# A layer's expert weights on one core: moved side work, and doubles that change places at every second step

## The reference, cut to what matters

```python
def _moe(h, w_router, b_router, w_gate, w_up, w_down):
    logits = (h @ w_router).astype(jnp.float32) + b_router.astype(jnp.float32)
    top_vals, top_idx = lax.top_k(logits, TOP_K)
    wts = jax.nn.softmax(top_vals, axis=-1)
    combine = jnp.sum(jax.nn.one_hot(top_idx, N_EXPERTS, dtype=jnp.float32) * wts[..., None], axis=-2)
    combine = combine.astype(h.dtype)
    out = jnp.zeros_like(h)
    for e in range(N_EXPERTS):
        out = out + combine[..., e:e + 1] * _swiglu(h, w_gate[e], w_up[e], w_down[e])
    return out
```

## Time and profile before

| what | value |
|---|---|
| median of 3 runs | 1944.58 us (1942.08 to 1948.06) |
| the profiled execution's own time | 1946.7 us |
| its span in the profile | 1944.6 us |
| TensorE busy | 1879.9 us, 97% |
| VectorE, ScalarE busy | 955.1 us, 743.2 us |
| moved by DMA | 488.11 MB, mean 251 GB/s |

### The profile page before, as it was taken

One profiled execution on the slowest core, in us unless ns is written; L12 is line 12 of the kernel. 1 busy time (PEld: TensorE's weight loads), 2 busy tenths in 40 slices (PEclk: granted clock), 3 DMA queues, 4 the chain that ended last, 5 costly groups with the idle time before them and its releaser, 6 DMA issues.

```text
span 1944.6 us, 30547 instructions
## 1 busy us (share of the span) xinstructions
PE 1879.9 (97%) x12510; PEld 1455.2 (75%) x12510; DVE 955.1 (49%) x1313; ACT 743.2 (38%) x931; POOL 127.6 (7%) x171
## 2 busy tenths in 40 slices
PE   7999999998999999999999998999999999999997
PEld 5999999997999988999999974356556655455444
DVE  4467554555444445575545642255455544333333
ACT  4434333445434334343334441244444443333222
POOL 2200001400000003000014010000000000000000
PEclk9999999999999999999999999999999999999999
DMA  9635356673666645533566739999999999899986
GB/s 359 212 122 162 112 171 178 201 271 88 192 211 184 231 125 166 160 109 103 163 195 206 238 142 365 384 387 380 402 395 387 381 409 373 306 324 353 349 311 232
DMA packets 275921, 488.11 MB, mean 251 GB/s; under 512 B 16951, under 2 KB 169657, under 8 KB 275778
## 3 DMA queue, kind: packets, MB, share of 16 engines
q1 hardware_dynamic: 266368, 458.02, 67.7%
q0 software_dynamic: 9392, 28.05, 4.7%
q10 hardware_dynamic: 18, 0.04, 0.0%
HBM read 473.45 MB, written 12.59 MB: 250 GB/s over the span
## 4 chain that ended last, share of the span: by engine, by line
PE 80%; DMA 8%; DVE 5%; SPq 2%; ACT 2%; issue 2%; POOL 1%; DVEq 0%; ACTq 0%; POOLq 0%
PE ps L2571 12%; PE ps L2572 11%; PE ps L2617 10%; PE ps L3291 6%; PE ps L3300 3%; DMA mraw<-in_w_exp_up 3%; PE ps L2641 3%; PE ps L3220 2%; PE ps L3443 2%; PE ps L2650 2%; PE ps L2538 2%; DMA mraw<-in_w_exp_down 2%; PE ps L3336 2%; PE ps L3250 2%; PE ps L3337 2%
## 5 line engine op out<-in xcount | busy, mean ns | idle before, releaser
L820 DVE TENSOR_TENSOR wlo<-raw,whi 128x1024 fp32r<-128x1024 f32 x244 | 288.9, 1211 | 310.7 <-ACT whi L1853 309.8
L2571 PE MATMUL ps<-h1h,whi 128*128 128x320 f32 x1248 | 384.8, 321 | 7.5 <-DVE h1l L927 3.9
L2572 PE MATMUL ps<-h1l,whi 128*128 128x320 f32 x1248 | 370.0, 309 | 0.0
L1853 ACT ACTIVATE whi<-raw 128x1024 fp32r<-128x1024 f32 x244 | 248.0, 1046 | 118.7 <-PE ps L2961 44.9
L2571 PEld LDWEIGHTS ps<-h1h,whi 128*128 128x128 f32 x1248 | 234.7, 188 | 23.6 <-issue 17.6
L1427 DVE TENSOR_TENSOR mhi<-mraw,mhi 128x2048 fp32r<-128x2048 f32 (+1 forms) x70 | 151.9, 2170 | 171.0 <-ACT mhi L2151 167.9
L2572 PEld LDWEIGHTS ps<-h1l,whi 128*128 128x128 f32 x1248 | 234.9, 188 | 0.2 <-issue 0.2
L2617 PE MATMUL ps<-h1h,wlo 128*128 128x320 f32 x1248 | 209.4, 310 | 0.0
L2151 ACT ACTIVATE mhi<-mraw 128x2048 fp32r<-128x2048 f32 (+1 forms) x70 | 127.0, 1814 | 205.0 <-DMA mraw<-in_w_exp_up 138.3
L2617 PEld LDWEIGHTS ps<-h1h,wlo 128*128 128x128 f32 x1248 | 189.0, 188 | 0.8 <-issue 0.8
L1658 DVE TENSOR_TENSOR mhi<-mraw,mhi 128x2048 fp32r<-128x2048 f32 (+1 forms) x35 | 75.9, 2168 | 120.6 <-PE ps L3342 115.4
(11 more groups left out here) (522 smaller groups left out, 3020.6 us busy)
## 6 DMA issues: line engine op xcount, KB each, us to landing
mraw<-in_w_exp_down SPq DMA_DIRECT2D x176, 512.0 KB, 10.2
raw<-in_w_in SPq DMA_DIRECT2D x128, 512.0 KB, 3.9
mraw<-in_w_exp_gate SPq DMA_DIRECT2D x123, 512.0 KB, 9.8
mraw<-in_w_exp_up SPq DMA_DIRECT2D x123, 512.0 KB, 11.3
raw<-in_w_ada SPq DMA_DIRECT2D x64, 512.0 KB, 3.9
mraw<-in_w_exp_gate SPq DMA_DIRECT2D x59, 384.0 KB, 7.3
mraw<-in_w_exp_up SPq DMA_DIRECT2D x59, 384.0 KB, 9.6
pause<-in_w_ada SPq DMA_DIRECT2D x32, 512.0 KB, 6.9
```

The source lines that it names most:

```text
L820: V.tensor_tensor(WLO[:, u % RAW_UNITS, 0:w], RAW[:, u % RAW_UNITS, 0:w], WHI[:, h % HI_UNITS, 0:w].bitcast(F32), ALU.subtract).then_inc(l ...
L1853: A.activation(WHI[:, h % HI_UNITS, 0:w], RAW[:, u % RAW_UNITS, 0:w], ACT.Copy).then_inc(hi_made, 1)
L2571: M.matmul(out_, w, v[0], start=start, stop=False, skip_group_check=True)
L2572: M.matmul(out_, w, v[1], start=False, stop=False, skip_group_check=True)
```

## The change

1. `triple_order`: `ahead` is 61 in place of 60. From pair 10 of the wide expert on, some narrow pairs stand one place earlier, and narrow pair 58 comes before wide pair 34. Behind wide pair 34 then stand the narrow pairs 59 to 69, where before it was 58 to 69.
2. `triple_units`: the combine units 5, 6 and 7, until now behind places 8, 9 and 10 of `ORDER`, stand behind places 10, 11 and 12.
3. ScalarE: the four GT copies are in a function that is called at pair 12 of job 0.
4. The doubles: at odd steps the wide pair comes first and the narrow one second, on TensorE and in the loads (narrow, wide, wide, narrow, and so on). The numbers that tell slots and counts follow.

```diff
-def triple_order(ahead=60):
+def triple_order(ahead=61):
...
-        units[3 + d].append(("combine", d))
+        units[3 + d if d < 5 else 5 + d].append(("combine", d))
...
-        return self.job * PAIRS - len(ASIDE) + self.stride * (p + 1) - 1
+        return self.job * PAIRS - len(ASIDE) + self.stride * (p + 1) - 1 - p % 2
...
-        return self.job * PAIRS - len(ASIDE) + self.stride * p
+        return self.job * PAIRS - len(ASIDE) + self.stride * p + p % 2
...
+            def wide_place(q):
+
+                return (q + q // 2) % 2
+
             def slot_free(both, q):
 
-                if q % 2:
+                if wide_place(q):
                     sp.wait_ge(m_lo, both.order * PAIRS + (q // 2 + 1))
                 else:
                     sp.wait_ge(m_used, both.job * PAIRS + (q + 1))
...
-                    load_pair((both.job * PAIRS - len(ASIDE) + q) % RAW_RING, experts[q % 2], q // 2)
+                    load_pair((both.job * PAIRS - len(ASIDE) + q) % RAW_RING, experts[wide_place(q)], q // 2)
...
-            act.wait_ge(hd_stored, 16 * TT)
-            act.wait_ge(sem("gt_in"), 1)
...
+            def gate_rows_out():
+
+                act.wait_ge(hd_stored, 16 * TT)
+                act.wait_ge(sem("gt_in"), 1)
...
+                    if side is SIDE_FIRST and p == 12:
+                        gate_rows_out()
...
+                    for part in (wide_, narrow) if p % 2 else (narrow, wide_):
+                        part()
```

More of the change, by code:

```diff
@@ L2185, in _ @@
             A.activation(*first_fill(0), ACT.Copy).then_inc(xe_out, 1)
-            act.wait_ge(hd_stored, 16 * TT)
-            act.wait_ge(sem("gt_in"), 1)
[L2188 to L2192, removed]
+            def gate_rows_out():
+                act.wait_ge(hd_stored, 16 * TT)
+                act.wait_ge(sem("gt_in"), 1)
+                for h in range(2):
+                    A.activation(GT[:, 0, 512 * h:512 * h + 512], PS[:, GT_BANKS[0][h], :], ACT.Copy)\
+                        .then_inc(sem("gt_out"), 1)
+                for h in range(2):
+                    A.activation(GT[0:TS, 1, 512 * h:512 * h + 512], PS[HALF * h:HALF * h + HALF, GT_BANKS[1][h], :],
+                                 ACT.Copy).then_inc(sem("gt_out"), 1)
             def high_turn(s, k, base, made):
@@ L3210, in gate_up_both @@
                     hi_, lo_ = MHI[:, p % BOTH_HI, :], MHI[:, BOTH_HI + p % BOTH_LO, :]
-                    raw_ = half_ready(p)
                     if p == 4:
@@ L3216, in gate_up_both @@
                         pe.wait_ge(prod_made, both.tile(t - 2))
[L3217 to L3237, removed]
+                    def narrow():
+                        raw_ = half_ready(p)
+                        for n in range(2):
+                            k = 2 * (p % 4) + n
+                            for j in range(2):
+                                ins = M.matmul(PS[HALF * j:HALF * j + HALF, half_, 0:w], XEF2[:, k, :],
+                                               raw_[:, (2 * j + n) * w:(2 * j + n + 1) * w], start=(k == 0),
+                                               stop=(k == KD - 1), skip_group_check=True)
+                        ins.then_inc(m_used, 1)
@@ new lines, in wide_ @@
+                    def wide_():
+                        pe.wait_ge(m_hi, order * PAIRS + (p + 1))
+                        for n in range(2):
+                            k = 2 * (p % 4) + n
+                            for j, bank in enumerate((gate_, up_)):
+                                s = slice((2 * j + n) * w, (2 * j + n + 1) * w)
+                                M.matmul(PS[:, bank, 0:w], XEH[:, k, :], hi_[:, s], start=(k == 0), stop=False)
+                                M.matmul(PS[:, bank, 0:w], XEL[:, k, :], hi_[:, s], start=False, stop=False)
+                        pe.wait_ge(m_lo, order * PAIRS + (p + 1))
+                        for n in range(2):
+                            k = 2 * (p % 4) + n
+                            for j, bank in enumerate((gate_, up_)):
+                                s = slice((2 * j + n) * w, (2 * j + n + 1) * w)
+                                ins = M.matmul(PS[:, bank, 0:w], XEH[:, k, :], lo_[:, s], start=False,
+                                               stop=(k == KD - 1))
+                        ins.then_inc(m_used, 1)
@@ L3248, in down_both @@
                         turned_in(0, kf, turn2_at)
[L3249 to L3267, removed]
+                    def narrow():
+                        raw_ = half_ready(p)
+                        for kf in kfs:
+                            for h in range(2):
+                                ins = M.matmul(PS[HALF * h:HALF * h + HALF, down[2], :], GTF2[:, kf, :],
+                                               raw_[:, (2 * (kf % 2) + h) * 512:(2 * (kf % 2) + h + 1) * 512],
+                                               start=(kf == 0), stop=(kf == KF - 1), skip_group_check=True)
+                        ins.then_inc(m_used, 1)
@@ new lines, in wide_ @@
+                    def wide_():
+                        pe.wait_ge(m_hi, order * PAIRS + (p + 1))
+                        for kf in kfs:
+                            for h in range(2):
+                                s = slice((2 * (kf % 2) + h) * 512, (2 * (kf % 2) + h + 1) * 512)
+                                M.matmul(PS[:, down[h], :], GTH[:, kf, :], hi_[:, s], start=(kf == 0), stop=False)
+                                ins = M.matmul(PS[:, down[h], :], GTL[:, kf, :], hi_[:, s], start=False, stop=False)
+                        if p == PAIRS - 1:
+                            ins.then_inc(m_tile, 9 * both.stride)
+                        pe.wait_ge(m_lo, order * PAIRS + (p + 1))
+                        for kf in kfs:
+                            for h in range(2):
+                                s = slice((2 * (kf % 2) + h) * 512, (2 * (kf % 2) + h + 1) * 512)
+                                ins = M.matmul(PS[:, down[h], :], GTH[:, kf, :], lo_[:, s], start=False,
+                                               stop=(kf == KF - 1))
+                        ins.then_inc(m_used, 1)
@@ L3269, in both_pe @@
+                    for part in (wide_, narrow) if p % 2 else (narrow, wide_):
+                        part()
                 for p in range(PAIRS):
-                    ins = gate_up_both(p) if p < GPAIRS else down_both(p)
-                    ins.then_inc(m_used, 1)
+                    if p < GPAIRS:
+                        gate_up_both(p)
+                    else:
+                        down_both(p)
                     side_both(both, p, before, then)
```

## The result

The changed kernel takes 1935.21 us (median of 4 runs, 1933.79 to 1938.42), the kernel before 1944.59 us (median of 4 runs, 1942.08 to 1948.06). The ratio is 0.9948, with a 95% interval from 0.9934 to 0.9963: 9.4 us less, where the prediction said 9.0. The profiled execution of the changed kernel has a span of 1936.39 us (its own time is 1938.42), that of before 1944.60.

A forecast was written before the change was run, and what follows sets the result against it. DMA was taken to bound the doubles, leading TensorE by 0.1 to 0.5 us a step, and TensorE's gaps to cost time elsewhere. The terms 6.3 + 1.6 + 1.1 + 0 = 9.0 us gave 1935.6 us, range 1930.5 to 1941.5.

The forecast's parts named there:

- the likeliest case: Whole kernel: the time comes as forecast, 1935.6 us, own range 1932 to 1939; chance 0.60.
- DMA sets the pace of the doubles, so the new order gives nothing: Doubles: TensorE's saving of about 0.35 us per two steps is hidden behind DMA; 0 us, bounds -0.6 and +0.6.
- Part 1: GT copies in job 0: moving them removes TensorE's 4.08 us gap and the slow clock behind it; 6.3 us, bounds 3.5 and 6.9.
- third term: Job 0, within the GT copies' gain: some 0.4 us for the modelled end of the last matmul before the gap.
- Part 2: Triple, combine 5 to 7: moving them removes a 1.63 us gap at place 9; 1.6 us, bounds 1.3 and 1.8.
- Level within 0.1 us: Triple, behind wide pair 4: combine 6's wait for combine 5, 2.3 + 0.5 us against 0.44 + 0.44 + 1.87.
- Part 3: Kernel's end, ahead 61: pair 59 no longer waits 1.73 us for its copy; 1.1 us, between 0.4 and 1.73.
- the idle tenth of the window 1880 to 1889, 0.9 us: Near the triple's end: DMA's idle time there, 0.9 us, is what can move the last loads earlier.
- The sign that I named: End, profile after: no gap at pair 59, but one or two of the last narrow pairs waiting for DMA.
- The stall is swallowed: Job 0: the queue doesn't use the freed time, so the GT copies give only 0 to 3.5 us; chance 0.20.
- Changing places pays: Doubles: with quicker transfers or TensorE as bound, 34 double steps at 0.35 us give 12 us, 1923.7; chance 0.07.
- The queue runs dry at odd steps: Doubles: late narrow releases empty the queue, 0.5 us lost at each of 34 odd steps, 17 us, 1952.6; chance 0.08.

The follow-up runs named there:

- order_only: Only the new order in the doubles, with its loads, added to the kernel before: 1944.75 us, ratio 0.9990.
- two_more: Changed kernel with combine 5 to 7 behind wide pairs 4, 5 and 6 and GpSimd's extra-expert row loads behind the last narrow pair: 1939.54 us, ratio 0.9970.
- gt_only: Only the GT copies moved behind pair 12's silus, against the kernel before: 1939.67 us, ratio 0.9963.
- combine_only: Only combine 5 to 7 moved to places 10 to 12, against the kernel before: 1943.13 us.
- ahead_only: Only ahead 61 in place of 60, against the kernel before: 1941.93 us.
- three_only: GT copies, combine 5 to 7 and ahead 61 changed in the kernel before, without the new order in the doubles: 1937.22 us, ratio 0.9956.
- light kernels: Kernel before and changed kernel, each with the narrow pairs' second transfer in the doubles cut from 512 KB to 64 KB: 1929.41 and 1915.81 us.
- light_before: Kernel before with the second transfer of each narrow pair in the doubles cut from 512 KB to 64 KB: 1929.41 us.
- ring5_after: Changed kernel, each load of the doubles also waiting for release of the pair five places ahead, two slots less of stock: 1944.14 us.
- ring4_after: Changed kernel, each load of the doubles also waiting for release of the pair four places ahead, three slots less of stock: 1972.89 us.

## Why the prediction was right

The time, 1935.21 us, lies 0.4 us from the forecast 1935.6, and the likeliest case is the one that came. That it is so close is partly luck: the interval of the ratio allows a gain of 7.2 to 12.8 us, and in the profiles the three parts and the doubles give 5.99 + 1.10 + 1.49 - 0.04 = 8.5 us. Parts 1 and 2 came out smaller than forecast and part 3 larger. Step by step:

- **DMA sets the pace of the doubles, so the new order gives nothing** (taken 0, bounds -0.6 and +0.6). Shown for the doubles, within their scatter. With the new order the doubles last 362.79, 362.31 and 362.11 us (after, order_only, two_more), without it 362.75, 362.49, 362.55, 362.63 and 362.11 (before, gt_only, combine_only, ahead_only, three_only): the means are 362.40 and 362.51. The light kernels show that DMA is what hides the saving. The Trainium skill's 435 GB/s (DMA: Bandwidth & Descriptors, "Where 436 GB/s comes from") was not reached in any window of the doubles: with whole transfers and the whole ring they stayed at 386 to 409.
- **Part 1, 6.3 us.** Measured 5.99 in both pairs that isolate it (before and after; before and gt_only). That is 4.08 and 1.77, with 0.14 left for the third term, 0.4 for the modelled end of a matmul. Of this only the sum is measured. But the second is not a constant: over the seven kernels with the gap it makes the stage 6.0 to 7.3 us longer, 6.5 in the mean. The room in DMA was enough: nothing was given back in the doubles. In the kernel, pair 19 is seven pairs behind pair 12 and not "some ten"; the copies are hidden there all the same.
- **Part 2, 1.6 us.** Measured 1.00 (alone) and 1.10. The gap went, but the term was mis-sized by 0.5 to 0.6. "Level within 0.1 us" came out as a wait of 0.15, and combines 6 and 7 now stand each alone behind a narrow pair, at 0.63 us each (0.34 + 0.15 + 0.14), where one behind a wide pair costs about 0.43. Combine 6 stood behind a narrow pair before too, but beside a transpose; so two more narrow pairs now have a unit behind them. I had counted a move as free of cost because no work is added.
- **Part 3, 1.1 us.** Measured 1.49 in the changed kernel, 1.70 alone and 1.80 beside parts 1 and 2 without the new order (three_only: 24.56 + 1.44 against 27.80). The step that was mis-sized is what can move the last loads: "the idle tenth of the window 1880 to 1889, 0.9 us". The two windows ahead of it are idle by 0.20 and 0.13 of 10 us, 3.3 us more. The 0.9 were also read from DMA's share, where part 1 read its room from the rate: 279 GB/s against 393 makes some 2.6 us of that window alone (an estimate, since the rate of gate and up is lower). So the end had more room than I gave it. The sign that I named, one of the last pairs waiting for DMA, did come: 0.24 us at pair 68. But it isn't there in three_only, which has the same triple and 24.56 us at the end. The end is at the edge, and in single executions it waits or doesn't. With the rows for the extra experts loaded late (two_more) it lasts 24.56 us too, and pairs 66 to 69 land 4.2 to 5.5 us ahead of their use.
- **What no term had:** 1.2 us in the output and 1.5 at the start. Both are scatter from one execution to the next. A profile pair alone would have shown 8.21 us and tempted one to give the 1.20 to the change.
- **The rivals.** *The stall is swallowed*: refuted by gt_only. *Changing places pays*: its condition is right (it takes TensorE as the bound), its price of 12 us is not; it would be 3.7, since side units stand at the very turns where the kinds no longer change. *The queue runs dry at odd steps*: did not happen, and its rule is refuted too. I let the new order lose from the point where a later release exceeds the stock. With the stock cut from 6.6 to some 1.2 us it lost 3.1 us more than the old order, not 20 to 60, and with none left by that sum it lost 1.7 us less. A likely reason is that of two narrow releases the one comes late and the next early, so on average the queue gets its slots at the same rate; this I have not isolated.

What stays open is whether the new order gives something that the stages don't show. Both comparisons of whole times lean that way: order_only lies 2.4 us under the kernel before beside it, and the ratio of the changed kernel is 0.9948 where that of three_only is 0.9956. Against it, the doubles of the kernels with the new order are not shorter beyond their scatter (362.40 and 362.51 us in the mean), the changed kernel has the longer doubles and end of the two (by 0.7 and 0.3 us), and the start and the output scatter by more than 1 us each. There is one profile of each kernel, which isn't enough to decide over 1 to 2 us.

## What to carry to other kernels

Cut two traces at the same instructions before explaining a total: here the stages repeat to 0.01 us where nothing waits, so there single profiles tell apart effects of 0.1 us that whole-kernel times can't, and the scatter shows itself as two or three places that no edit touched. Where an engine waits for DMA, a stage scatters by more (0.7 us in the doubles). A stall on a kernel bound by DMA is worth its length only as far as the transfers idle with it, and a reordering that saves the engine behind DMA is worth little or nothing until the bytes fall. A low rate at a full share isn't room: cut the window finer before counting on it. Moving a unit is not free: price what stands ahead of it and behind it, and count how many units then hang on the same VectorE queue, or the knot only changes place.

## What the runs showed of the hardware

- A gap of TensorE has a price beyond its length, and it varies. After gaps of 4.08 us the next 16 matmuls took 5.35 to 6.67 us in place of 3.58 (before, light_before), after one of 1.98 us 5.35 (two_more), with windows at 0.50 to 0.69 of the full clock; after gaps of 1.63 and 1.73 us (the triple of before) they took the usual time, in the output gaps of 2.01 and 2.64 us were followed by 0.66 in the one execution and 1.00 in the other (before, after); and at the start of ONE's down stage a gap of 2.47 us was followed by 0.72 from 1380 to 1385 (order_only) and one of 2.46 us by 1.00 (after). That the clock falls behind idle time and comes back with work agrees with the Trainium skill (TensorE: Matmul & The Clock Gate, "What's actually happening"); that the same gap costs 1.8 us in one execution and 3.1 in another was new to me.
- How much stock the queue of transfers needs depends on the stage. While gate and up are read, 386 GB/s held with medians of 6.6 and 8.2 us from issue to landing in place of 11.0 and 11.5 (ring5_after, 512 KB transfers), and fell to 368 at 4.8 and 6.2 us (ring4_after). While down is read, the same shorter ring already took it from 408 or 409 GB/s to 393 to 399.
- Transfers with rows of 4 KB (down) ran at 408 to 409 GB/s, those with rows of 2 KB (gate and up) at 386 to 387, each constant over tens of us. That the row length sets this was not isolated.
- DMA's share can be full while the rate isn't: 1.06 at 251 GB/s from 1907 to 1911 in the kernel before, with GpSimd's last row loads in flight beside the weights. With those loads moved to the output (two_more) the rate was 411 GB/s from 1900 to 1909, and the last two weight transfers took 8.1 and 10.1 us from issue to landing in place of 12.3 and 13.4.
